# One ring of SBUF for the routing stage and the expert stage of a decoder layer

## The reference

```python
x = layer_norm(DN_ALPHA * x + gt * mix, ln_g[layer, 0], ln_b[layer, 0])
h = x * (1 + sc2) + sh2
ff = moe_ffn(h, router_w, router_b, moe_w_in[layer], moe_w_out[layer])
x = layer_norm(DN_ALPHA * x + gt2 * ff, ln_g[layer, 1], ln_b[layer, 1])

def moe_ffn(h, router_w, router_b, w_in, w_out):
    aff = sigmoid(h @ router_w)
    ...
    gt, up = split(x_pad[tok] @ w_in[e], 2)
    return (silu(gt) * up) @ w_out[e]
```

## Time and profile before

| | |
|---|---|
| time of three runs | 4426.47 us median (4415.01 to 4433.32) |
| the profiled execution, its own time | 4414.47 us |
| its span, first to last instruction | 4412.7 us |
| mean granted TensorE clock, share of full speed | 0.862 |
| data moved by DMA | 853.21 MB, 193 GB/s over the span |

### The profile page before, as it was taken

How to read it: one execution, slowest core, us unless ns; L and a number is a source line. 1 busy time by engine, 2 the same in 40 slices (tenths; PEclk the granted TensorE clock), 3 DMA queues, 4 the chain that set the end, 5 groups by cost and what they waited for, 6 DMA issues and landing times. The chain is left out here.

```text
span 4412.7 us, 70051 instructions
## 1 busy us (share of the span) xinstructions
PE 3351.8 (76%) x26856; PEld 1901.0 (43%) x26857; DVE 1580.4 (36%) x3082; ACT 1012.4 (23%) x1546; POOL 680.4 (15%) x453
## 2 busy tenths in 40 slices
PE   5379996799985964899791589994886964888880
PEld 1156653688874431333230344553775431232330
DVE  0210010576665851223126421002555851222226
ACT  0000011323221211343232000112553211233332
POOL 0000001423231211000004000000540321000005
PEclk9689987899996976999995698997887976999995
DMA  9982222112113418999984421117554409899974
GB/s 400 359 324 77 77 86 94 60 37 72 43 62 107 148 44 336 386 368 382 354 319 181 140 78 57 67 53 153 135 105 149 128 34 340 349 406 353 382 300 186
DMA packets 340553, 853.21 MB, mean 193 GB/s; under 512 B 68942, under 2 KB 153952, under 8 KB 334585
## 3 DMA queue, kind: packets, MB, share of 16 engines
q1 hardware_dynamic: 256908, 529.12, 34.7%
q0 software_dynamic: 65408, 257.77, 14.7%
q10 hardware_dynamic: 18000, 62.91, 3.6%
HBM read 672.77 MB, written 181.19 MB: 194 GB/s over the span
## 5 line engine op out<-in xcount | busy, mean ns | idle before, releaser
L1888 PE MATMUL moe_ps_h<-moe_wi,moe_xT 128*64 x1472 | 667.8, 613 | 177.9 <-DVE moe_lane L2026 98.1
L1889 PE MATMUL moe_ps_h<-moe_lane,moe_xT 128*64 128x512 f32 x1472 | 667.8, 613 | 0.0
L1888 PEld LDWEIGHTS moe_ps_h<-moe_wi,moe_xT 128*64 128x64 f32 x1472 | 204.4, 142 | 599.3 <-issue 599.3
L2446 PE MATMUL qkv_ps<-qkv_hh,qkv_wr 128*128 128x512 f32 (+1 forms) x1152 | 385.3, 491 | 22.1 <-DVE qkv_qsT L2396 19.5
L1888 PE MATMUL moe_ps_y<-moe_wo,moe_hT 128*64 x768 | 350.0, 610 | 21.1 <-ACT moe_lane L1963 21.1
L395 PE MATMUL mix_ps<-mix_mix,mix_wr 128*128 128x344 f32 x1152 | 337.2, 456 | 35.3 <-issue 22.0
L1889 PE MATMUL moe_ps_y<-moe_lane,moe_hT 128*64 128x512 f32 x768 | 350.0, 610 | 0.0
L1963 ACT ACTIVATE moe_lane<-moe_wi 128x1024 f32 x190 | 198.5, 1053 | 641.4 <-SPq L1850 425.2
L2026 DVE COPY moe_lane<-moe_wi 128x1024 f32 x190 | 127.8, 690 | 475.8 <-SPq L1850 231.9
L2446 PEld LDWEIGHTS qkv_ps<-qkv_hh,qkv_wr 128*128 128x128 f32 x1152 | 194.0, 195 | 213.6 <-issue 190.7
L395 PEld LDWEIGHTS mix_ps<-mix_mix,mix_wr 128*128 128x128 f32 x1152 | 220.7, 192 | 151.4 <-issue 38.7
(11 more groups left out here) (379 smaller groups left out, 5485.0 us busy)
## 6 DMA issues: line engine op xcount, KB each, us to landing
moe_wi<-in_moe_w_in_dram SPq DMA_DIRECT2D x64, 4096.0 KB, 19.4
moe_wo<-in_moe_w_out_dram POOLq DMA_DIRECT2D x64, 2048.0 KB, 16.8
ada_w<-in_ada_w_dram SPq DMA_DIRECT2D x32, 1536.0 KB, 36.4
moe_X<-t_xs_d ACTq DMA_DIRECT2D x52, 512.0 KB, 7.6
t_xs_d<-mix_z POOLq DMA_DIRECT2D x1, 25600.0 KB
t_proj_d<-mix_ev POOLq DMA_DIRECT2D x48, 516.0 KB
t_ysl_d<-moe_y ACTq DMA_DIRECT2D x48, 512.0 KB
wkv_raw<-t_proj_d SPq DMA_DIRECT2D x40, 516.0 KB
```

The costliest lines, as they stand in the source:

```text
L1888: pe.matmul(out[column(0), half], lhsT[:, k, column(0)], rhs, start=start and i == 0, stop=stop and i == 1)
L1889: ins = pe.matmul(out[column(1), half], lhsT[:, k, column(1)], lane[:, q % LANE, i], start=start and i == 0, stop=stop and i == 1)
L2446: ins = pe.matmul(ps[n % 2][:, s, 0:w], wr[:, n % 4, k, :], hh[:, 0, k, s * 512:s * 512 + w], start=(k == 0), stop=(k == KC - 1))
```

## The change

Three things are changed.

1. `NBLK` goes from 48 to 34, so the zeros written in `phase_mix` shrink from 50 to 36 blocks in `xs_d` and from 32 to 18 in `ysl_d`.
2. A class `Experts` owns the identity and a ring of three experts for one layer, `w_in` (3 x 4096 KB) and `w_out` (3 x 2048 KB), and lives over both `phase_post` and `phase_moe`. The large buffers of `phase_post` (`wo`, `mod`, `x`, `ln`, `x1`, `z`, `zt`, and `O`, `zs` or `bg`) become parts of that ring; `cmp_` becomes a part of `ta`.
3. ACT, in `phase_post`, issues the loads of the first three experts into each part of the ring when the buffers in it have been used for the last time. `phase_moe` loads from expert 3 on, announces the first three from the new semaphores, and no longer loads the identity.

```diff
-NBLK = 48
+NBLK = 34
...
-def phase_post(nc, T, layer):
+def phase_post(nc, T, layer, E):
...
-        wo = A.sb("wo", [P, KC, D])
+        wo = E.part("w_in", 1, 0, KC, D)
...
-        mod = A.sb("mod", [P, 2, 3, D])
-        ln = A.sb("ln", [P, 2, D])
-        zt = A.sb("zt", [P, 2, KC, P])
+        mod = E.part("w_in", 2, 0, 2, 3, D)
+        x = E.part("w_in", 2, 6 * D, 2, D)
+        ln = E.part("w_out", 1, 0, 2, D)
+        x1 = E.part("w_out", 1, 2 * D, 2, D)
         if layer:
-            O = A.sb("O", [P, 2, NG3, H * W1])
+            O = E.part("w_in", 0, 0, 2, NG3, H * W1)
+            zt = E.part("w_out", 2, 0, 2, KC, P)
+            z = E.part("w_out", 2, 2 * D, 2, D)
...
         else:
-            z = A.sb("z", [P, 3, D])
-            bg = A.sb("bg", [P, 2, KC, P])
+            z = E.part("w_out", 2, 0, 3, D)
+            zt = E.part("w_out", 0, 0, 2, KC, P)
+            bg = E.part("w_out", 0, 2 * D, 2, KC, P)
...
                     act.dma_start(T["x1_d"][rows(t), :], x1[:, t % 2]).then_inc(s_x1[t % 2], 16)
+                    if t == 0:
+                        E.load(act, "w_out" if layer else "w_in", 0)
+                    if layer and t == TT - 3:
+                        dv_.wait(act, f"cz{TILES - 1}")
+                        pe_.wait(act, f"zh1{TT - 1}")
+                        E.load(act, "w_in", 0)
+                    if t == TT - 1:
+                        pe_.wait(act, f"mm{TT - 1}")
+                        E.load(act, "w_in", 1)
+                        E.load(act, "w_out", 2 if layer else 0)
...
+                po_.wait(act, f"xm{TT - 1}")
+                E.load(act, "w_in", 2)
+                if not layer:
+                    E.load(act, "w_out", 2)
                 ac_.wait(act, f"lg{TT - 1}")
                 act.activation(aff[:], lg[:], ACT.Sigmoid).then_inc(s_aff, 1)
                 act.wait_ge(s_x1[0], 16 * (TT // 2 + 1))
                 act.wait_ge(s_x1[1], 16 * (TT // 2))
+                E.load(act, "w_out", 1)
...
+    def load(self, eng, name, e, sems=None):
+        out = self.ring[name][:, e % RING]
+        src = self.weights[name][e].rearrange("(k p) n -> p k n", p=P)
+        eng.dma_start(out.rearrange("p (k n) -> p k n", k=src.shape[1]), src).then_inc((sems or self.loaded[name])[e % RING], 16)
...
+        def announce(eng, name, sems, e, ready):
+            if e < RING:
+                eng.wait_ge(E.loaded[name][e], 16)
+            else:
+                eng.wait_ge(sems[e % RING], 16 * (e // RING))
+            eng.sem_inc(ready, 1)
...
-                sp.dma_start(ident[:], T["k_ident"]).then_inc(s_k, 16)
                 for e in range(NE):
                     if e == RING:
-                        sp.wait_ge(s_k, 48)
+                        sp.wait_ge(s_k, 32)
                     if e >= RING:
                         sp.wait_ge(s_ind, past(sp, e - RING))
-                    sp.dma_start(wi[:, e % RING], W_IN[e].rearrange("(k p) n -> p k n", p=P)).then_inc(s_wi[e % RING], 16)
+                        E.load(sp, "w_in", e, s_wi)
                     if e:
-                        sp.wait_ge(s_wi[(e - 1) % RING], 16 * ((e - 1) // RING + 1))
-                        sp.sem_inc(s_in, 1)
+                        announce(sp, "w_in", s_wi, e - 1, s_in)
...
-    phase_post(nc, T, 0)
-    phase_moe(nc, T, 0)
+    with Experts(nc, T, 0) as E:
+        phase_post(nc, T, 0, E)
+        phase_moe(nc, T, 0, E)
```

More of the change, by code:

```diff
@@ L1 @@
+import math
 from contextlib import ExitStack
@@ L1192, in phase_post @@
             cs = A.sb("cs", [P, 2, H])
-            z = A.sb("z", [P, 2, D])
-            zs = A.sb("zs", [P, D])
-        else:
-            z = A.sb("z", [P, 3, D])
-            bg = A.sb("bg", [P, 2, KC, P])
+            zs = E.part("w_in", 0, 2 * NG3 * H * W1, D)
+        else:
+            z = E.part("w_out", 2, 0, 3, D)
+            zt = E.part("w_out", 0, 0, 2, KC, P)
+            bg = E.part("w_out", 0, 2 * D, 2, KC, P)
             gp = A.sb("gp", [P, 2, KC])
             gs = A.sb("gs", [P, 2, H])
-        x = A.sb("x", [P, 2, D])
         t1 = A.sb("t1", [P, D])
-        x1 = A.sb("x1", [P, 2, D])
         xm = A.sb("xm", [P, TT, D])
@@ L1229, in phase_post @@
         th = A.sb("th", [P, 17])
-        cmp_ = A.sb("cmp", [P, NE, 16])
+        cmp_ = ta[:].rearrange("p t k e -> p (t k e)")[:, 0:NE * 16].rearrange("p (e j) -> p e j", e=NE)
         nu = A.sb("nu", [P, NE])
@@ L1758, in post_consts @@
     out["k_valid"] = np.ascontiguousarray(tok < NT).astype(one)
-    out["k_dummy"] = np.stack([48 * P + i, 49 * P + i], 1).astype(one)
+    out["k_dummy"] = np.stack([NBLK * P + i, (NBLK + 1) * P + i], 1).astype(one)
     e = np.arange(NE)
@@ L1763, in post_consts, with __init__, __enter__, __exit__ @@
     return out
-def phase_moe(nc, T, layer):
-    W_IN, W_OUT = T["moe_w_in"][layer], T["moe_w_out"][layer]
+class Experts:
+    def __init__(self, nc, T, layer):
+        self.nc, self.tag, self.layer, self.ctx = nc, f"experts{layer}", layer, ExitStack()
+        self.weights = {"w_in": T["moe_w_in"][layer], "w_out": T["moe_w_out"][layer]}
+    def __enter__(self):
+        self.ctx.__enter__()
+        buffer = lambda name, shape: self.ctx.enter_context(self.nc.sbuf_tensor(f"{self.tag}_{name}", shape, F32))
+        self.ident = buffer("ident", [P, P])
+        self.ring = {"w_in": buffer("w_in", [P, RING, KC * 2 * DE]), "w_out": buffer("w_out", [P, RING, KE * D])}
+        self.loaded = {name: [self.nc.alloc_semaphore(f"{self.tag}_{name}_loaded{e}") for e in range(RING)] for name in self.ring}
+        return self
+    def __exit__(self, *a):
+        return self.ctx.__exit__(*a)
+    def part(self, name, slot, at, *shape):
+        a = self.ring[name][:, slot, at:at + math.prod(shape)]
+        dims = "abc"[:len(shape)]
+        return a.rearrange(f"p ({' '.join(dims)}) -> p {' '.join(dims)}", **dict(zip(dims, shape)))
+    def load(self, eng, name, e, sems=None):
+        out = self.ring[name][:, e % RING]
+        src = self.weights[name][e].rearrange("(k p) n -> p k n", p=P)
+        eng.dma_start(out.rearrange("p (k n) -> p k n", k=src.shape[1]), src).then_inc((sems or self.loaded[name])[e % RING], 16)
+def phase_moe(nc, T, layer, E):
     with Pool_(nc, f"moe{layer}") as A:
-        ident = A.sb("ident", [P, P])
+        ident = E.ident
         tab = A.sb("tab", [1, 1 + NE], I32)
@@ L1777, in phase_moe @@
         xT = A.sb("xT", [P, 2, KC, P])
-        wi = A.sb("wi", [P, RING, KC, 2 * DE])
-        wo = A.sb("wo", [P, RING, KE, D])
+        wi = E.ring["w_in"][:].rearrange("p r (k n) -> p r k n", k=KC)
+        wo = E.ring["w_out"][:].rearrange("p r (k n) -> p r k n", k=KE)
         lane = A.sb("lane", [P, LANE, 2, 512])
@@ L1790, in phase_moe @@
         s_k = A.sem("constants_loaded")
+        A.sems += E.loaded["w_in"] + E.loaded["w_out"]
         s_wi = [A.sem(f"w_in_loaded{j}") for j in range(RING)]
@@ L1826, in bodies @@
         def bodies(eng):
-            eng.wait_ge(s_k, 48)
+            eng.wait_ge(s_k, 32)
             return eng.value_load(tab[0:1, 0:1], min_val=NE // 4, max_val=NU // 4)
@@ L1857, in _ @@
                     if e == RING:
-                        pool.wait_ge(s_k, 48)
+                        pool.wait_ge(s_k, 32)
                     if e >= RING:
                         wait_at(pool, s_outd, past(pool, e - RING) + 2, s_nil)
-                    pool.dma_start(wo[:, e % RING], W_OUT[e].rearrange("(k p) n -> p k n", p=P)).then_inc(s_wo[e % RING], 16)
+                        E.load(pool, "w_out", e, s_wo)
                     if e:
[L1863 to L1866, removed]
+                        announce(pool, "w_out", s_wo, e - 1, s_out)
+                announce(pool, "w_out", s_wo, NE - 1, s_out)
             @block.tensor
@@ L2864, in yoco_step @@
     phase_attend(nc, T)
-    phase_post(nc, T, 1)
-    phase_moe(nc, T, 1)
+    with Experts(nc, T, 1) as E:
+        phase_post(nc, T, 1, E)
+        phase_moe(nc, T, 1, E)
     phase_combine(nc, T, 1)
```

9 lines of the change are left out of this document (4 added, 5 removed).

## The result

| | before | the change |
|---|---|---|
| median of the runs compared | 4421.56 us (4415.01 to 4433.32) | 4375.54 us (4358.68 to 4391.87) |
| ratio, 95% interval | | 0.9893 (0.9848 to 0.9938) |
| profiled execution, its own time | 4414.47 us | 4371.82 us |

The change makes the kernel 1.1% faster: 46.0 us by these medians, where 54.9 was forecast.

What follows compares the result with a forecast made beforehand. PE bounds phase_mix, idling for a late store; phase_moe opens waiting for expert 0, then PE and DMA near their limits. 15.4 + 40.2 + 2.0 - 1.3 - 1.4 = 54.9 us off the 4426.47 median: 4372, range 4340 to 4402.

Steps and rivals of the forecast that it cites:

- Fewer zeros: phase_mix: 14.68 MB less written lets the store land earlier; PE's 13.3 us gap and slow restart go, gain 15.4 us.
- Expert 0 and the identity: Start of phase_moe: no wait for expert 0's announcement, 40.2 us for both layers; no identity load, 2.0 us.
- The six loads: phase_post: in layer 0 the last five loads run 1.3 us into the scatter, charged as cost; layer 1's end before it.
- The issues: phase_post: four ACT issues ahead of the sigmoid or an exponential, at 0.35 us each, cost 1.4 us.
- the held queue: Rival in phase_post: seven ACT issues held ahead of the sigmoid, 12.0 us each, cost 84 us; 4454, chance 0.04.
- The stalls in the loop: Expert loop of phase_moe: stalls later in the loop stay as long as before; fewer and shorter ones would prove it wrong.
- The stream as the bound: Rival in phase_moe: the weights' stream sets the pace, each layer saves 48.4 us, gain 109.5; 4317, chance 0.06.
- The start given back in the ring: Rival in phase_moe: the first stall grows by what the start won, 12.7 us gain stays; 4414, chance 0.05.
- The loads that meet the scatter: Rival in phase_post: loads share the engines with the scatter, 60 us more over both layers; 4430, chance 0.05.

Runs made afterwards that it cites:

- the two pairs of profiles: The changed kernel and its twin with the larger zero fill, profiled twice; the second time side by side: 4357.41 and 4375.43 us.
- sig_first: The changed kernel with ACT's sigmoid ahead of the loads that stood between the last logits and it: 4363.10 us, and 4361.91 in another comparison.
- zeros48: The changed kernel with only the smaller zero fill undone (50 and 32 blocks again): 4371.32 us; run again, 4375.43.
- only0: The changed kernel with only expert 0 loaded inside phase_post, experts 1 and 2 at the start of phase_moe by SP and POOL: 4364.72 us.
- late_loads: The changed kernel with the last five loads of layer 0, four of layer 1, issued only when the scatter begins: 4418.22 us.

## Why the prediction was right

*The total.* 4375.5 lies 3.5 us from the forecast of 4372, and that it is so near is in part luck: the gain fell 8.9 us short of the sum, and the kernel before took 4.9 us less in the comparison than the 4426.47 from which the forecast subtracts. Of the sum of 54.9, three comparisons found 46.0, 56.1 and 46.5.

*Fewer zeros, 15.4.* Right in mechanism and size: 15.7 and 14.7 us at the end of the 24 groups in the two pairs of profiles, 14.4 over the stage against the kernel before, 18.0 by the medians of the second pair.

*Expert 0 and the identity, 42.2.* Right: 20.8 us in layer 0 and 20.7 in layer 1, 41.5 in all; 1.0 and 0.9 of it lie ahead of the transposes, as forecast for the identity. The idle time ahead of the loop was forecast at about 8 us and is 8.85 and 8.75.

*The six loads, -1.3.* Right to expect them done in the routing window, at 410 GB/s in its first 10 us, and a scatter no longer than before. The last of their packets ends 0.9 us ahead of the scatter, not 1.3 us into it, but only because the held issue had put the scatter back: in sig_first, where it isn't put back, they last 2.7 us into it. Here the Trainium skill, page "DMA: Bandwidth & Descriptors", section "Specifications", has about 358 GB/s as one core's limit; the 410 GB/s after stand against it as the 390 before did.

*The issues, -1.4.* This term was mis-sized. The step took 0.35 us for an issue from the earlier trace rows and kept the held queue for a rival, argued away because the second pair follows the first by 11 us. In these 11 us the queue had not drained enough. One issue was held 3.61 us ahead of the sigmoid and cost 3.8; `phase_post` grew by 4.3 and 1.1 us, 5.4 in all, in place of 2.7 (1.3 + 1.4). The rival's mechanism was real, but with one held issue on the path, not seven.

*The stalls in the loop "as long as before".* Right for the waits, 98.1 and 98.2 us, or 136.9 and 138.5 with those that ACT's copies end. What the sum left out is that PE's clock after each stall is not the same in each run. In the last third of layer 0 both kernels have one short stall (3.09 us before, 3.77 after). The product that ends it and the window behind it, before and after:

```profile
2251.22 0.64 PE L1888 MATMUL moe_ps_y<-moe_wo,moe_hT 128*64 x1 [3.09 <-ACT moe_lane L1963]
...
2251.00:2259.00 8.00, 7.78 (x38) 2.88 (x40) 4.60 (x7) 4.11 (x6) 0.00 (x0) 1.00 1.03 410
```

```profile
2228.48 1.11 PE L1939 MATMUL moe_ps_y<-experts_w_out,moe_hT 128*64 x1 [3.77 <-ACT moe_lane L2014]
...
2228.00:2236.00 8.00, 7.52 (x24) 2.37 (x26) 3.82 (x6) 3.47 (x5) 0.00 (x0) 0.65 1.03 410
```

PE ran at its full 2.4 GHz behind the stall before, and began again at 1.2 after (a granted clock of 0.65 in the mean): 24 products in place of 38 in 8 us. In that profile the loop of layer 0 took 629.0 us from the first product to the last, 621.5 before; in the seven profiles of the changed kernel, zeros48 and sig_first, which have the same code there, it took 619 to 629, with 50 products of the loop above 0.9 us in the shortest and 86 in the longest. These 7.5 us are most of the 12.2 that the first profile of the changed kernel lacks of the sum. As the same code varies by 10 us, they need not be a cost of the change; but there is one profile of the kernel before only, so that it has no part in them isn't shown.

*The rivals.* The stream as the bound (4317) fell with only0. The start given back in the ring (4414) did not happen. The loads that meet the scatter don't in this kernel, but late_loads shows that the price put on it was near: 55 us against sig_first where 60 were forecast, 4418 for 4430.

## What to carry to other kernels

A prefetch is worth the wait that it ends, not its bytes: one expert's weights, in place when the stage begins, gave nearly all that three gave, because later loads were released by PE anyway. Look for the stretch in which the DMA engines are empty, and for what follows it: the same loads were free in the routing window and cost their whole gain 28 to 39 us later, beside the scatter. When a compute engine issues large loads, put what the chain waits for ahead of the issue, since a full queue holds the engine.

## What was not expected of the hardware

An empty queue took two loads of 4096 KB at once (1.02 us for both issues in layer 0), and in layer 1 of late_loads one of 2048 KB behind them after 1.32 us. The next issue was held: three of 2048 KB took 36.32 us in layer 0 while the scatter shared the engines. Every hold of 3 us and more ended when 6.7 to 7.7 MB were still to move on the queue, the held load included, counted from the packets. The same loads from two engines' queues were not held (0.39 and 0.41 us), with the DMA engines as full.

Single runs differ with PE's clock: of the changed kernel's first four, 4358.68 us goes with a mean granted clock of 0.869 and 4391.87 with 0.862. Two places show it. The same products took 0.54 or 0.30 us in one group of `phase_mix`, by kernel and not by run as far as the profiles show; and behind a stall of 3.09 us in the expert loop PE ran at 2.4 GHz in one profile, behind one of 3.77 us at 1.2 in another. What decides it these runs don't show.
